# Twenty-two gate panels of two layers: one full-precision product replaced by three fp32r products with an accumulating transfer

## The reference

```
proj = h @ w_in                      # 256 x 1024 times 1024 x (many columns)
(a, q, k, v, qi, ki, wi, hq, hf, hi, hg, gates) = split(proj)
y_a = pool_mixer(a, ...)             # windowed means, small product
y_b = sparse_attention(q, k, v, qi, ki, wi, rel_bias)   # top-64 keys by an index score
y_c = hgrn2(hq, hf, hi, hg, ...)     # gated linear recurrence
g = sigmoid(gates.reshape(B, S, 3, D_MODEL))
merged = g[:, :, 0] * (y_a @ wb0) + g[:, :, 1] * (y_b @ wb1) + g[:, :, 2] * (y_c @ wb2)
return merged @ w_out
```

## Time and profile before

| | |
|---|---|
| median of 3 runs | 2983.58 us (2980.86 to 2990.65) |
| profiled execution, its own time | 2986.41 us |
| span of its trace | 2984.6 us |
| TensorE busy | 2741.6 us (92%) |
| VectorE busy | 1933.1 us (65%) |
| ScalarE busy | 1090.5 us (37%) |
| GpSimd busy | 183.1 us (6%) |
| granted TensorE clock, mean share of full | 0.973 |

### The profile page before, as it was taken

One profiled execution on the slowest core, in us unless ns is written; L12 is line 12 of the kernel. 1 busy time (PEld: TensorE's weight loads), 2 busy tenths in 40 slices (PEclk: granted clock), 3 DMA queues, 4 the chain that ended last, 5 costly groups with the idle time before them and its releaser, 6 DMA issues.

```text
span 2984.6 us, 48702 instructions
## 1 busy us (share of the span) xinstructions
PE 2741.6 (92%) x18394; PEld 2328.0 (78%) x18394; DVE 1933.1 (65%) x3304; ACT 1090.5 (37%) x1387; POOL 183.1 (6%) x85
## 2 busy tenths in 40 slices
PE   3999988999999889999999958999999899889998
PEld 3998877899999887799977835687744777668887
DVE  6776555677778656565756464577776676664881
ACT  2434332443543333254464542333300644442211
POOL 0000000000000000000013300244300000000000
PEclk9999999999999999999999989999999999999999
DMA  8775624677576453346512110122367222113442
GB/s 304 273 290 219 254 100 163 220 266 287 207 260 249 170 197 113 137 160 219 194 67 66 37 64 29 57 99 89 115 250 287 83 71 71 49 65 115 153 167 72
DMA packets 105950, 469.13 MB, mean 157 GB/s; under 512 B 7004, under 2 KB 56744, under 8 KB 57896
## 3 DMA queue, kind: packets, MB, share of 16 engines
q1 hardware_dynamic: 105768, 466.67, 43.3%
HBM read 465.58 MB, written 1.06 MB: 156 GB/s over the span
## 4 chain that ended last, share of the span: by engine, by line
PE 34%; DVE 11%; DVEq 7%; ACT 3%; issue 3%; DMA 1%; ACTq 1%; SPq 0%
PE accs L826 6%; DVEq L2818 4%; PE accs L672 4%; PE accs L687 3%; PE accs L688 3%; PE accs L689 3%; DVE arena L2795 3%; PE accs L1215 2%; PE accs L1216 2%; PE accs L1217 2%; DVE arena L2103 1%; PE accs L1348 1%; ACT arena L76 1%; PE mix L873 1%; PE mix L1272 1%
## 5 line engine op out<-in xcount | busy, mean ns | idle before, releaser
L687 PE MATMUL accs<-normed_r,arena_r 128*128 128x256 f32 (+2 forms) x1864 | 586.4, 315 | 14.3 <-DVEq L2148 6.9
L689 PE MATMUL accs<-normed_r,panel_r 128*128 128x256 f32 (+2 forms) x1872 | 585.7, 313 | 0.0
L688 PE MATMUL accs<-arena_r 128*128 128x256 f32 x2069 | 584.5, 283 | 0.0
L86 DVE TENSOR_TENSOR panel_r<-panel,arena_r 128x1024 fp32r<-128x1024 f32 (+1 forms) x295 | 387.2, 1312 | 174.1 <-ACTq L1468 129.8
L1467 ACT ACTIVATE arena_r<-panel 128x1024 fp32r<-128x1024 f32 (+1 forms) x292 | 330.9, 1133 | 374.0 <-DMA panel<-w 190.4
L687 PEld LDWEIGHTS accs<-normed_r,arena_r 128*128 128x128 f32 (+1 forms) x1864 | 350.9, 188 | 51.0 <-issue 11.7
L688 PEld LDWEIGHTS accs<-arena_r 128*128 128x128 f32 x2069 | 389.3, 188 | 1.2 <-issue 0.2
L689 PEld LDWEIGHTS accs<-normed_r,panel_r 128*128 128x128 f32 (+1 forms) x1872 | 351.0, 187 | 24.2 <-issue 0.8
L672 PE MATMUL accs<-normed,panel 128*128 128x256 f32 x1536 | 345.2, 385 | 6.8 <-ACTq L475 3.1
L2795 DVE SCALAR_TENSOR_TENSOR arena<-accs,vectors,arena 128x189 f32<-128x189 f32 (+2 forms) x704 | 279.5, 428 | 95.8 <-issue 63.9
L672 PEld LDWEIGHTS accs<-normed,panel 128*128 128x128 f32 x1536 | 292.2, 192 | 54.4 <-issue 4.6
(11 more groups left out here) (406 smaller groups left out, 4708.7 us busy)
## 6 DMA issues: line engine op xcount, KB each, us to landing
panel<-w SPq DMA_DIRECT2D x250, 1024.0 KB, 5.0
panel<-w SPq DMA_DIRECT2D x48, 1408.0 KB, 8.1
cond_panel<-wc SPq DMA_DIRECT2D x57, 1024.0 KB, 5.9
normed<-wc SPq DMA_DIRECT2D x43, 1024.0 KB, 6.8
arena<-wc SPq DMA_DIRECT2D x19, 1024.0 KB, 5.5
residual<-xs SPq DMA_DIRECT2D x2, 1024.0 KB, 9.7
residual<-wc SPq DMA_DIRECT2D x1, 1024.0 KB, 13.0
residual<-crows SPq DMA_DIRECT2D x2, 512.0 KB, 9.3
```

Of the source, the lines that this page charges most:

```text
L86: i = self.eng.tensor_tensor(*a, **k)
L687: pe.matmul(out, hi[:, k, 0:m], src_hi(k), start=clear and k == 0, stop=False, skip_group_check=True)
L688: pe.matmul(out, hi[:, k, 0:m], src_lo(k), start=False, stop=False, skip_group_check=True)
L689: mm = pe.matmul(out, lo[:, k, 0:m], src_hi(k), start=False, stop=last and k == n - 1, skip_group_check=True)
```

## The change

Gates 1 to 11 of each layer are multiplied in three fp32r products; gate 0 stays as it was. For each of these 22 panels:

1. ScalarE (`gate_split`) copies the panel, rounded, to a buffer `gate_hi` (even panels: the half of H; odd ones: the second cond slot), and then writes the negated rounded panel over the panel itself.
2. GpSimd issues a transfer that reads the same 1 MB again from device memory and adds it onto the negated panel, which leaves the low part. Its semaphore is `gate_low_landed`.
3. TensorE runs 32 products with the hi part (input hi and lo), waits for the transfer, and runs 16 with the low part.

ScalarE splits panels 1 and 2 at the start of pool, and panel u+2 behind the evacuation of gate u, for u from 1 to 9. Since the cond slots are now in use until gate 11, the cond loads of the branch stage go behind all its panel loads. A second edit makes ScalarE's first exp wait for the third count of `cond_done` in place of a semaphore of its own, and drops two semaphore signals.

```diff
+        gate_hi = [H_r[:, :, 0:T], cond_slot1_r[:, :, :]]
...
+        gate_low = [sem(f"gate_low_landed{i}") for i in range(2)]
...
+                        if g.name == "branch0":
+                            continue
...
+                if g.name == "branch0":
+                    for i in range(g.n):
+                        load_cond(g.name, 0, i)
...
             def gate(l, *panels):
+                g = G[f"gate{l}"]
                 for u in panels:
-                    features(G[f"gate{l}"], 0, u, lambda k: H[:, k, lat], T)
+                    if u == 0:
+                        features(g, 0, u, lambda k: H[:, k, lat], T)
+                        continue
+                    b = acc_open(g, 0, u)
+                    w, rest = gate_hi[u % 2], slots_r[(g.p0 + u) % SLOTS]
+                    pe.wait_ge(S("gate_parts"), 2 * (g.n - 1) * l + 2 * u - 1)
+                    for j in range(2):
+                        out = acc[b][:, j * T:j * T + T]
+                        for k in range(KD):
+                            pe.matmul(out, w[:, k, j * P:j * P + P], mix_hi[:, k, :], start=(j == 0 and k == 0), stop=False, skip_group_check=True)
+                            pe.matmul(out, w[:, k, j * P:j * P + P], mix_lo[:, k, :], start=False, stop=False, skip_group_check=True)
+                    pe.wait_ge(gate_low[u % 2], 16 * (u // 2 + (6 * l + 1 if u % 2 else 5 * l)))
+                    for j in range(2):
+                        for k in range(KD):
+                            mm = pe.matmul(acc[b][:, j * T:j * T + T], rest[:, k * PANEL + j * P:k * PANEL + j * P + P], mix_hi[:, k, :],
+                                           start=False, stop=(k == KD - 1), skip_group_check=True)
+                    mm.then_inc(ready[b], 1)
...
+            for l in range(DEPTH):
+                g = G[f"gate{l}"]
+                for u in range(1, g.n):
+                    pool.wait_ge(S("gate_parts"), 2 * (g.n - 1) * l + 2 * u)
+                    pool.dma_start(slots_r[(g.p0 + u) % SLOTS][:, 0:KD * PANEL], w8[g.row0 + u:g.row0 + u + 1, :, :].rearrange("a p n -> p (a n)"),
+                                   accum_op=ALU.add).then_inc(gate_low[u % 2], 16)
...
+            def gate_split(l, u):
+                g = G[f"gate{l}"]
+                s = (g.p0 + u) % SLOTS
+                act.wait_ge(landed[s], 16 * ((g.p0 + u) // SLOTS + 1))
+                w = slots[s][:, 0:KD * PANEL].rearrange("p (k c) -> p k c", k=KD)
+                rest = slots_r[s][:, 0:KD * PANEL].rearrange("p (k c) -> p k c", k=KD)
+                act.activation(gate_hi[u % 2], w, ACT.Copy).then_inc(S("gate_parts"), 1)
+                act.activation(rest, w, ACT.Copy, scale=-1.0).then_inc(S("gate_parts"), 1)
...
             def gate(l, *panels, func=ACT.Copy):
                 for u in panels:
                     evac(G[f"gate{l}"], 0, u, 0, gates[:, 2 * u:2 * u + 2, :], both, func)
+                    if u >= 1 and u + 2 < G[f"gate{l}"].n:
+                        gate_split(l, u + 2)
 
             def pool(l):
+                act.wait_ge(S("cond_done"), (CARRY["branch0"][0], CARRY["mixout1"][0])[l])
+                gate_split(l, 1)
+                gate_split(l, 2)
                 gate(l, 0, 1)
...
-            act.wait_ge(S("lb_diff"), 1)
+            act.wait_ge(S("cond_done"), 3)
```

More of the change, by code:

```diff
@@ L2571, in decays @@
                     if p == 3:
-                        dve.drain().then_inc(S("ml_decays"), 1)
+                        dve.drain()
                 def normalise(n, tok):
@@ L2865, in _ @@
                 dve.tensor_tensor(small[:, 4 * i:4 * i + 4], lb[i], small[:, 8:12], ALU.subtract)
-            dve.drain().then_inc(S("lb_diff"), 1)
+            dve.drain()
             for i in range(2, 5):
```

## The result

The changed kernel takes 3031.1 us, the kernel before 2986.4 (four runs of each, in the same session): a ratio of 1.0149, interval 1.0125 to 1.0173, or 45 us slower. The forecast was slower by 22 us; the side was right, the size half of what came. The range left for it, 2989 to 3042, holds the measured time; the forecast's own, 2998 to 3016, does not. In the profiled executions the spans are 3033.2 and 2984.6 us, 48.6 apart.

The account below looks back on a forecast made before the run. TensorE's gates were taken to set the pace in pool and hgrn, tied with VectorE and ScalarE in attention. Per layer 4.6 + 5.6 - 1.5, two layers 17.4, plus clock 4.8: +22 on 2983.6, 3005.6 us; range 2989 to 3042.

Parts of the forecast that it names:

- Landing, taken as 9 us: Adding transfer, from the end of the split to TensorE's wait being released: 9 us, midway between bounds of 5.0 and 13.
- the slow rival: Transfers land at 13 us: per layer 20.3, with the clock +45, 3029 us; chance 15%.
- the quick rival: Transfers land in 5 to 7 us and gate 2 isn't cold: 5.7 per layer, +11, 2995 us; chance 20%.
- Split, 3.9 us: ScalarE's two copies of 128x2048 for each panel, with the drain between: 3.9 us a split, 86 us for 22.
- gate, 1.1 us less: TensorE's 48 products take 5.67 us against 6.75 for a full-precision gate: 1.1 us won each, 24 us for 22 gates.
- Pool, +4.6 a layer: Pool ends at 20.7 us in place of 16.1, its scaling queued behind the split of panel 3: +4.6.
- Attention +5.6, with the clock +8.0 a layer: Attention's copy of transposed block 1, queued behind panel 8's split, comes 5.6 us later; gate 2 at half clock adds 2.4.
- Hgrn, -1.5 a layer: In hgrn gates 8 and 11 win 1.1 us each, some is lost again: 1.5 us shorter a layer.
- Rival: TensorE's passes decide (24 us faster): ScalarE's copies find room and the stages shrink with TensorE's products: up to 24 us faster, 2960 us; chance 5%.
- What costs nothing: Later cond loads of the branch stage, 22 MB of extra traffic and the first exp's third `cond_done` count: no cost.

Follow-up runs that it names:

- the passes alone: Kernel before with gates 1 to 11 in three passes over one rounded panel per layer, no second copy, transfer or other split: 2980.4 us, ratio 0.9976.
- the filled version: The changed kernel with 128x128 products that nobody reads put into TensorE's new idle times in both layers: 3018.6 us, ratio 1.0107.
- the copies alone: Kernel before, gates at full precision, plus ScalarE's 22 pairs of copies at the change's places with nobody waiting for them: 3028.5 us, ratio 1.0141.

## Why the prediction was right in its side and wrong in its size

- *Landing, taken as 9 us.* Right. Where TensorE waited for it: split 1 ended at 367.90 and the third pass of gate 1 was released at 377.08, 9.2; gate 5's pair is 418.37 and 428.11, 9.7; in layer 1 they took 9.0 and 10.0. Gate 10's in layer 0 took 12.7; in layer 1, after at most 9.6, it was there when TensorE came. The forecast's estimate from the Trainium skill ("DMA: Bandwidth & Descriptors", anatomy of a DMA by the software path), 6.8 us for two reads, is under the measured 8.8; the rule behind it (a reducing transfer reads twice, "Collectives: The Full Stack") fits the direction, 8.8 against 5.0 for a plain load. The slow and the quick transfer were both out as the usual case. That the slow rival's time, 3029, is next to the measured 3031 is luck: it rests on landings of 13 us. For a landing of 5 us the forecast's own times give about +3.9 in attention and not +4.9 (exps of block 0 to 36.7, then evacuation, split 7 and the rest), which would make the quick rival some +9; nothing else hangs on it.
- *Split, 3.9 us; gate, 1.1 us less.* Right: 1.92 a copy, and a gate of 48 products at the full clock covers 5.9 to 6.0 us to its last result (in the passes alone) against 7.17.
- *Pool, +4.6 a layer.* Measured +6.3 and +6.4, 3.4 of the missing 23 us. The scaling came at 21.3 us, not 19.5. In layer 0, 0.9 of that is the start of split 1, which stood 1.05 us for its panel's load, 0.2 the landing, and some 0.5 the third pass, partly at half the clock behind its wait (2.56 for 2.06); in layer 1 the third pass took 3.64. The pool product ran slow too (1.91 for 1.03), but ended 3 us ahead of the scaling and cost nothing.
- *Attention +5.6, with the clock +8.0 a layer.* **This is the step that failed.** Measured +14.2 and +15.5, 13.6 of the missing 23 us. The queue was followed correctly in kind: relus behind split 4, exps of block 1 behind split 7 (at 51.2 us into the stage, not 43.1), the copy behind split 8 (59.2, not 51.0). What was left out is that the products behind these new idle times run at half the clock as well, and not those of gate 2 alone: the clock was charged once, 2.4 us, and the filled version shows 6.9 us a layer.

  The forecast's own times show where the difference grew in layer 0 (how late each is, without the 2.4 of the clock): gate 2 ends +3.3 us, gates 3 to 5 start +4.0, split 5 ends +5.4, the third pass of gate 5 starts +6.2, the exps of block 1 +8.1, the copy +8.2, the stage's end +8.6. The slow products on this way are the index products (3.09 for 1.71), the first passes of gate 2 (5.74 for 4.05), the logits (3.43 for 2.49), the first passes of gate 3 (5.29 for 4.05), the third pass of gate 5 (3.78 for 2.06) and the last product with v (1.90 for 1.58): 7.3 us in all.

  The Trainium skill ("TensorE: Matmul & The Clock Gate", Part 1) puts the warming-up under 1% of a typical kernel's span; the 12.6 us won by filling are 0.4% of this one, which agrees, but they are more than a quarter of what the change moved. With 6.9 in place of 2.4 the sum is 22 + 9 = 31. The rest of attention's miss is some 2.3 us a layer; the landing in front of gate 5's third pass, 9.7 for 9, is 0.7 of it, and what makes the remainder stays open. So 14 of the 45 us lie outside this term: 4.6 in attention, 3.4 in pool, 6.1 in hgrn.
- *Hgrn, -1.5 a layer.* Wrong as well: measured +3.0 and +0.1, 6.1 of the missing 23. In layer 0 the third pass of gate 10 waits 3.23 us for the landing of 12.7 and takes 3.36 for 2.06; in layer 1 it doesn't wait. The forecast had this case (+2 with a landing of 13), as a rival's. The passes alone win 3.4 a layer here, the copies alone cost 2.1 and the landing 0.9; that does not add up to the measured +1.5, and the clock of this stage, 0.78 to 1.00 over these kernels, was not held still and may be what is missing.
- *Rival: TensorE's passes decide (24 us faster).* Dead. Even with no copies and no transfers the passes win 7 us: attention did not get shorter, and TensorE waited 6.51 us for VectorE there.
- *What costs nothing.* The moved condition loads and the third count are in all versions of the change, the passes alone among them, and that one is faster than before: no sign of a cost. From the end of hgrn in layer 0 to the pool of layer 1, where the condition loads stand, the kernels took 603.0 to 608.4 us, the kernel before 605.3. The extra traffic was not as light as its share suggested: it took the transfer engines' share in pool, attention and hgrn from 0.49, 0.36 and 0.29 to 0.90, 0.72 and 0.58. Plain loads came later by it (last section), but ScalarE waited at most 1.05 us for one.

The sum of the account: copies in ScalarE's queue +42 (13 of it TensorE's clock), passes -15 against that, landing +17. The terms hold in this order only: against the kernel before, the same passes are worth 7 us and not 15.

## What to carry to other kernels

Price work that is added to an in-order engine by what stands behind it, not by its busy share, and then go on one step: list the idle times that it opens on TensorE, and charge each with the half clock of the products behind it, here mostly 1 to 3 us for each wait of 3 to 6 us (one wait of 2.86 us cost nothing: 2.16 for 2.06). A window that shows more busy time for less work, with a granted clock below 1, is the sign; products that nobody reads, put into the wait, are the test. And put added work where nothing that its stage waits for is queued behind it: here three gates of eleven paid a little, eleven didn't.

## What the runs showed of the hardware

- A transfer of 1 MB that adds into its destination, issued by GpSimd, landed in 8.8 us in the median (7.9 to 12.3 in the change, the two of panel 2, issued 4 us behind those of panel 1, in 12.2 and 12.0), 10.8 in the version with six of them; plain loads of the same size took 5.0.
- The adding transfers hold up the plain loads beside them. Within the three stages the plain loads of 1 MB took 7.4 us (layer 0) and 7.1 (layer 1) in the median in the change, up to 12.0, and 4.9 in the version without transfers, at most 5.7.
- Filling 46 products of 128x128 a layer into waits made the kernel with the copies alone 13 us faster, although each takes 0.24 us of TensorE.
- Hgrn's length goes with its clock more than with the copies in it; which of the two moves the other these rows don't tell, though filling brought one layer from 0.87 to 1.00. With gates at full precision and 29.0 us of ScalarE's work it took 58.1 us at a granted clock of 1.00, 62.5 at 0.92 and 64.0 at 0.87; with the copies, 40.4 us of ScalarE's work, 60.3 and 61.9 at 0.97, and 68.8 to 69.2 at 0.85. One kernel has both lengths in its two layers (the copies alone, layers 0 and 1):
```profile
444.92:506.77 61.85, 50.87 (x656) 44.34 (x656) 32.68 (x51) 40.44 (x43) 0.00 (x0) 0.97 0.31 110
1195.29:1264.09 68.80, 57.22 (x657) 49.73 (x657) 32.65 (x51) 40.38 (x43) 0.00 (x0) 0.85 0.23 78
```
